# HGRN2 with a third operand buffer, and its steps spread differently over a head's four items

## The reference

```python
q = silu(q_raw) * DK ** -0.5
f = lb + (1 - lb) * sigmoid(z);  k = (1 - lb) * sigmoid(-z);  v = i_raw
b = cumsum(log f)                       # within a chunk
attn[t, s] = sum_d q[t, d] k[s, d] exp(b[t, d] - b[s, d])      # s <= t
o = attn @ v + (q * exp(b)) @ S         # S: state of the earlier chunks
o = rmsnorm(o, onorm_g);  y = o * silu(gate)
```

## Time and profile before

| | |
|---|---|
| median of 3 runs | 1422.78 us (1422.21 to 1424.14) |
| the profiled execution's own time | 1425.11 us |
| its span, first to last instruction | 1423.3 us |
| mean granted TensorE clock | 0.988 of full |
| TensorE matmul busy | 1303.7 us (92%), 5886 instructions |
| VectorE busy | 765.2 us (54%) |
| ScalarE busy | 639.7 us (45%) |
| GpSimd busy | 600.1 us (42%) |

### The profile page before, as it was taken

How to read it: one execution, slowest core, us unless ns; L and a number is a source line. 1 busy time by engine, 2 the same in 40 slices (tenths; PEclk the granted TensorE clock), 3 DMA queues, 4 the chain that set the end, 5 groups by cost and what they waited for, 6 DMA issues and landing times.

```text
span 1423.3 us, 16609 instructions
## 1 busy us (share of the span) xinstructions
PE 1303.7 (92%) x5886; PEld 1033.3 (73%) x5886; DVE 765.2 (54%) x1174; ACT 639.7 (45%) x988; POOL 600.1 (42%) x756
## 2 busy tenths in 40 slices
PE   0399889999999999999978988999999999999996
PEld 0277677788777777788857777778877777778884
DVE  6867884633555524534347778463355552454433
ACT  2245554544455334444335555454445533444531
POOL 3243333465232444445534333356523244454551
PEclk9999999999999999999989999999999999999998
DMA  9121111344223233333322111135422323333321
GB/s 366 45 75 60 59 45 59 104 157 131 83 68 110 91 108 100 103 126 104 104 83 74 60 58 49 57 104 162 132 77 67 111 94 111 98 102 123 105 103 59
DMA packets 46018, 139.70 MB, mean 98 GB/s; under 512 B 5744, under 2 KB 5744, under 8 KB 45680
## 3 DMA queue, kind: packets, MB, share of 16 engines
q1 hardware_dynamic: 28656, 102.65, 21.6%
q10 hardware_dynamic: 17280, 35.99, 7.9%
HBM read 136.52 MB, written 2.10 MB: 97 GB/s over the span
## 4 chain that ended last, share of the span: by engine, by line
PE 74%; DVE 14%; ACT 6%; issue 3%; DMA 1%; POOL 1%; ACTq 0%; DVEq 0%
PE ps_st L657 20%; PE ps_st L659 20%; PE ps_st L658 20%; PE ps_o L679 4%; PE ps_s L749 2%; PE ps_s L704 1%; PE ps_s L773 1%; DVE pro_acc L1125 1%; PE ps_w L758 1%; PE ps_misc L674 1%; ACT w_hi L833 1%; DVE t L1389 1%; DMA pro_w<-w_mod_first 1%; DVE h_lo L1394 1%; DVE hg_x L1334 1%
## 5 line engine op out<-in xcount | busy, mean ns | idle before, releaser
L570 POOL TENSOR_TENSOR w_lo<-raw,w_hi 128x256 fp32r<-128x256 f32 x744 | 587.9, 821 | 774.9 <-ACT w_hi L833 774.9
L657 PE MATMUL ps_st<-h_hi,w_hi 128*128 128x512 f32 x1008 | 413.4, 410 | 1.1 <-POOL w_lo L570 1.1
L659 PE MATMUL ps_st<-h_hi,w_lo 128*128 128x512 f32 x1008 | 395.0, 392 | 0.0
L658 PE MATMUL ps_st<-h_lo,w_hi 128*128 128x512 f32 x1008 | 394.2, 391 | 0.0
L657 PEld LDWEIGHTS ps_st<-h_hi,w_hi 128*128 128x128 f32 x1008 | 190.6, 189 | 48.5 <-issue 6.4
L658 PEld LDWEIGHTS ps_st<-h_lo,w_hi 128*128 128x128 f32 x1008 | 190.8, 189 | 43.7 <-issue 6.2
L659 PEld LDWEIGHTS ps_st<-h_hi,w_lo 128*128 128x128 f32 x1008 | 190.2, 189 | 41.3
L833 ACT ACTIVATE w_hi<-raw 128x1024 fp32r<-128x1024 f32 x186 | 195.2, 1051 | 27.6 <-PE ps_st L659 27.6
L855 ACT ACTIVATE gate_t<-gate_x 128x512 f32<-128x512 f32 x80 | 50.6, 632 | 248.3 <-DVE gate_x L1184 248.3
L1184 DVE TENSOR_SCALAR gate_x<-ps_st 128x512 f32<-128x512 f32 x80 | 55.2, 690 | 186.4 <-PE ps_st L659 186.0
L1532 DVE SCALAR_TENSOR_TENSOR mod_acc<-mod_w,cond,mod_acc 128x512 f32<-128x512 f32 x84 | 75.8, 902 | 21.2 <-DMA mod_w<-w_mod 18.5
(11 more groups left out here) (233 smaller groups left out, 1987.1 us busy)
## 6 DMA issues: line engine op xcount, KB each, us to landing
raw<-w_stream SPq DMA_DIRECT2D x186, 512.0 KB, 3.4
mod_w<-w_mod ACTq DMA_DIRECT2D x96, 256.0 KB, 2.7
pro_w<-w_mod_first ACTq DMA_DIRECT2D x16, 512.0 KB, 12.5
x<-x_t SPq DMA_DIRECT2D x4, 512.0 KB, 10.2
ret_decay<-decay ACTq DMA_DIRECT2D x2, 1024.0 KB, 5.9
out_t<-o_t SPq DMA_DIRECT2D x8, 256.0 KB, 2.1
cs<-cst SPq DMA_DIRECT2D x1, 906.5 KB, 4.8
pos_i<-positions ACTq DMA_DIRECT2D x1, 256.0 KB, 7.7
```

Of the source, the lines that this page charges most:

```text
L570: ins = nc.gpsimd.tensor_tensor(w_lo[:, i % RING, r], raw[:, i % RING, r], w_hi[:, i % RING, r].bitcast(F32), ALU.subtract)
L657: nc.tensor.matmul(dst[0:m, :], wh, hi, start=(k == 0), stop=False)
L658: nc.tensor.matmul(dst[0:m, :], wh, lo, start=False, stop=False)
L659: last = nc.tensor.matmul(dst[0:m, :], wl, hi, start=False, stop=(k == nk - 1))
```

## The change

The schedule of a head's steps is new. h is the head whose items run; what stands in a group before and after:

| group | before | after |
|---|---|---|
| f(h) | level steps 4, 5 of h-1 | level steps 2, 3 of h-1; value product of h-2 |
| q(h) | level steps 6, 7 of h-1; hz 1, 2; cross copy of h-1 | hz 1; level step 4 of h-1; hz 2; output of h-2 |
| i(h) | hz 3; value product of h-1; level steps 0, 1 of h; output of h-1 | hz 3; level steps 5, 6 of h-1 |
| g(h) | transposes of v; level steps 2, 3 of h | level step 7 and cross copy of h-1; transposes of v; level steps 0, 1 of h |

The steps of the last head run on through the first items of the latent attention. `hg_x` becomes three tiles, used by level modulo 3, and some tiles move to other addresses.

```diff
     def hg_first(h):
 
-        return ([("hg_lv", h - 1, 4), ("hg_lv", h - 1, 5)],
-                [("hg_lv", h - 1, 6), ("hg_lv", h - 1, 7), ("hz", h, 1), ("hz", h, 2), ("hg_cross", h - 1)],
-                [("hz", h, 3), ("hg_pv", h - 1), ("hg_lv", h, 0), ("hg_lv", h, 1), ("hg_out", h - 1)],
-                [("hg_v", h), ("hg_lv", h, 2), ("hg_lv", h, 3)])
+        return ([("hg_lv", h - 1, 2), ("hg_lv", h - 1, 3), ("hg_pv", h - 2)],
+                [("hz", h, 1), ("hg_lv", h - 1, 4), ("hz", h, 2), ("hg_out", h - 2)],
+                [("hz", h, 3), ("hg_lv", h - 1, 5), ("hg_lv", h - 1, 6)],
+                [("hg_lv", h - 1, 7), ("hg_cross", h - 1), ("hg_v", h), ("hg_lv", h, 0), ("hg_lv", h, 1)])
@@
     h = HG_HEADS
-    item("cq", 1)
-    s += hg_first(h)[0]
-    item("cq", 2)
-    s += [t for t in hg_first(h)[1] if t[0] != "hz"]
-    item("cq", 3)
-    s += [("hg_pv", h - 1)]
-    item("cq", 4)
-    s += [("hg_out", h - 1)]
+    tail = [[t for t in steps if t[0] not in ("hz", "hg_v") and t[1] < h] for steps in hg_first(h)]
+    for j in range(1, 5):
+        item("cq", j)
+        s += tail[j - 1]
     item("cq", 5)
+    s.append(("hg_pv", h - 1))
     item("ckv", 0)
     s.append(("cq_norm",))
     item("ckv", 1)
-    s.append(("cq_rest",))
+    s += [("hg_out", h - 1), ("cq_rest",)]
@@
-        hg_e, hg_x = at("hg_e", 12 * KB, [P, 2, SEQ]), at("hg_x", 16 * KB, [P, 2, SEQ])
-        hg_at = (at("hg_at0", 20 * KB, [P, CH, SEQ]), at("hg_at1", 40 * KB, [P, CH, SEQ]))
-        hg_kd = at("hg_kd", 28 * KB, [P, 3 * P])
+        hg_e, hg_x01 = at("hg_e", 12 * KB, [P, 2, SEQ]), at("hg_x", 16 * KB, [P, 2, SEQ])
+        hg_x2 = at("hg_x2", 87 * KB, [P, SEQ])
+        hg_x = (hg_x01[:, 0, :], hg_x01[:, 1, :], hg_x2[:])
+        hg_at = (at("hg_at0", 20 * KB, [P, CH, SEQ]), at("hg_at1", 28 * KB, [P, CH, SEQ]))
+        hg_kd = at("hg_kd", 85 * KB, [P, 3 * P])
@@
-        cq_raw, ckv_raw = at("cq_raw", 32 * KB, [P, CQT, SEQ]), at("ckv_raw", 44 * KB, [P, CKT, SEQ])
+        cq_raw, ckv_raw = at("cq_raw", 36 * KB, [P, CQT, SEQ]), at("ckv_raw", 79 * KB, [P, CKT, SEQ])
@@ tensor, level products
-                        left, right = (hg_x[:, n % 2, :], hg_x[:, n % 2, :]) if n < 5 else (hg_x[:, 0, :], hg_x[:, 1, :])
+                        left, right = (hg_x[n % 3], hg_x[n % 3]) if n < 5 else (hg_x[2], hg_x[0])
@@ vector, level_operands
-                    if 2 <= n < 5:
-                        dve.wait_ge(full[bank_of(("lv", h, n - 2))], e.use(full, ("lv", h, n - 2)))
+                    if 3 <= n < 5:
+                        dve.wait_ge(full[bank_of(("lv", h, n - 3))], e.use(full, ("lv", h, n - 3)))
                     elif n == 5:
+                        dve.wait_ge(full[bank_of(("lv", h, 2))], e.use(full, ("lv", h, 2)))
                         dve.wait_ge(full[bank_of(("lv", h, 3))], e.use(full, ("lv", h, 3)))
-                        dve.wait_ge(full[bank_of(("lv", h, 4))], e.use(full, ("lv", h, 4)))
-                    elif n < 2 and h:
+                    elif n < 3 and h:
                         dve.wait_ge(full[bank_of(("lv", h - 1, 5))], e.use(full, ("lv", h - 1, 5)))
...
```

More of the change, by code:

```diff
@@ L1331, in v @@
                             return t.rearrange("p (c s m) -> p c s m", s=2, m=LEVELS[n])
-                        V.tensor_tensor(v(hg_x[:, n % 2, :])[:, :, 0, :], v(hg_e[:, n % 2, :])[:, :, 0, :],
+                        V.tensor_tensor(v(hg_x[n % 3])[:, :, 0, :], v(hg_e[:, n % 2, :])[:, :, 0, :],
                                         v(k)[:, :, 0, :], ALU.mult)
-                        V.tensor_tensor(v(hg_x[:, n % 2, :])[:, :, 1, :], v(hg_e[:, n % 2, :])[:, :, 1, :],
+                        V.tensor_tensor(v(hg_x[n % 3])[:, :, 1, :], v(hg_e[:, n % 2, :])[:, :, 1, :],
                                         v(q)[:, :, 1, :], ALU.mult).then_inc(x_built, 1)
                     elif n == 5:
-                        V.tensor_tensor(hg_x[:, 0, :], hg_e[:, 0, :], k, ALU.mult)
-                        V.tensor_tensor(hg_x[:, 1, :], hg_e[:, 1, :], q, ALU.mult).then_inc(x_built, 1)
+                        V.tensor_tensor(hg_x[2], hg_e[:, 0, :], k, ALU.mult)
+                        V.tensor_tensor(hg_x[0], hg_e[:, 1, :], q, ALU.mult).then_inc(x_built, 1)
                     else:
```

## The result

The changed kernel takes 1446.03 us (median of 4 runs, 1444.91 to 1447.39) against 1422.52: the ratio is 1.0163, 95% interval 1.0146 to 1.0181. It is slower by 23.5 us, in the direction forecast (1430) but outside the range (to 1443), near the worst of the rivals (1445). The profiled execution took 1446.58 us, its span is 1444.7; the one of before 1425.11 and 1423.3. Beside the experiments the kernel before took 1423.70 to 1424.25 us, 1.2 to 1.7 more than beside the changed kernel, so a difference between the changed kernel and an experiment is uncertain by about that much, and reads low; the ratios to the kernel before are free of it.

A forecast was written before the change was run, and what follows sets the result against it. TensorE, busy 92% of the span, was taken as the bound, so reordering only changes its idle time. 42.4 - 37.4 - 6.3 + 8.4 = +7.1 us gave 1432.2, or 1430 on the median's scale; range 1414 to 1443.

The forecast's parts named there:

- the worst of the rivals: All six gaps trip the clock at the longest price and every pair is slow: +22, 1445 us; chance 0.15.
- Step 1, the buffer: Third operand tile for level operands: VectorE never waits there, so alone worth 0 (bounds -1 to +1 us).
- Step 2, the start: First level product of a layer: its 2.8 to 3.0 us wait shrinks to 0.9 per layer (bounds 0 to 3).
- Steps 3 and 4, the new wait and the loop: Transposes of v wait for w0's copy, looping over VectorE's drain of g: 7.2 us in heads 2 and 3, 5.3 in head 1.
- the walk: Engine-by-engine timing of head 2 or 3 from one drain of g to the next: cycle 39.8 against 37.4 us.
- The waits outside the loop: Per layer, 0.9 at the start and 0.6 for the tail's cross operands; also 1.2 at level 5 in head 1.
- My 42.4 us: TensorE's HGRN2 waits after the change, both layers, 21.2 per layer; bounds 16 to 48 us.
- the 37.4 for the kernel before: The 20 waits at level and cross-chunk products before, 34.4 us listed, plus about 0.15 us each for the emptied pipeline.
- Step 5, the slow rate: VectorE's base operands beside GpSimd's work, taken at the upper end; at the lower end a cycle is 0.9 us shorter.
- Step 6, the tail: Head 3's output moves to ckv1 from cq4, still several items ahead of its reader: 0 (bound 0 to +1).
- The clock: Half clock after TensorE's gaps: 6.3 us saved from three old drops, 8.4 added by four gaps in heads 2 and 3.
- +7.1: Net change forecast for the whole kernel in us, from new and old waits and clock losses.

The follow-up runs named there:

- e4: Kernel before with only the third operand tile and its waits, order unchanged: 1424.41 us, ratio 1.0006 to the kernel before.
- e3: Changed kernel with unused matmuls in TensorE's gaps ahead of the transposes of v and the cross products: 1438.34 us, ratio 1.0099 to the kernel before.
- e1: Changed kernel with the transposes of v written to bank o in place of w0: 1419.62 us, ratio 0.9966 to the kernel before.
- e5: Changed kernel with transposes of v moved from the fourth item's group to the next head's first, bank w0 kept: 1423.9 us, ratio 0.9995.
- e6: e5 with the output of h-2 listed behind the third item: 1414.29 us, ratio 0.9931 to the kernel before.
- e7: e5 with head 3's output directly behind its value product at cq5, ahead of the c_q norm: 1418.4 us, ratio 0.9959.
- e9: Changed kernel with transposes of v as in e5, head 3's output as in e7, output of h-2 behind the fourth item: 1401.18 us, ratio 0.9845.
- e10: Kernel before with unused matmuls in its gaps (level 4's product, cross products, a layer's first level product): 1420.71 us, ratio 0.9976.

## Why the prediction was right in direction and wrong in size

- *Step 1, the buffer*: right, 0 (e4).
- *Step 2, the start*: there is no listed wait at the first level product, where I took 0.9 (and 3.0 + 4 - 5.9 is 1.1, not 0.9); the clock stays full over 92 to 102. Right to about 1 us a layer.
- *Steps 3 and 4, the new wait and the loop*: right, and in size. At full clock the cycle is the 39.8 us of the walk (e3). Forecast were 2.5 and 4.7 us in heads 2 and 3, 4.1 in head 1, none in head 0, six waits on ScalarE's copy. Measured are 2.6 and 4.6 in layer 1, 4.1 in head 1; in layer 0 the wait on the copy is 3.2, because the cross products ahead of it run at half clock. e1 and e5 show the mechanism, e6 the part of the output chain.
- *The waits outside the loop failed in part.* Head 0's base operands I had not walked at all: 2.0 us a layer. The cross products of the last head, in the tail, I put at 0.6: 2.2. Against that the 0.9 of the start and the 1.2 at level 5 in head 1 did not come. My 42.4 us counts from the end of one matmul's pitch to the next start, like the 37.4 for the kernel before; on that scale the 14 listed waits of after are 42.9 + 14 times 0.15 = 45.0. So 2.6 us are missing, and the nearness of 42.4 and the listed 42.9 is luck.
- *Step 5, the slow rate*, is half in the trace: of the two base operands one, L1337, took 1.24 us, the other, L1336, 0.69. I took both at the upper end. In their place the exponents behind them (L1310) took 0.96 and not 0.56, so the stretch came to 2.8 us (158.41 to 161.25) where the walk has 2.9.
- *Step 6, the tail, failed.* "Still several items ahead of the product that reads it: 0". True of the product, but the step has other neighbours: its column sum takes bank misc ahead of the ckv norm's, and its root stands in ScalarE's queue behind the rest of the c_q norm. 4.8 us of waits and 3.0 us of half clock, about 8 us; e7 gives 7.9.
- *The clock was mis-sized.* For the kernel before I took 6.3 us from one trace; the filler gives 3.2. After, 8.4 were forecast for the heads and 7.7 found (9 by the ratios), but as six falls and not four, each cheaper than the 2.1 us I gave it: the sum came out by luck. The six falls are what the Trainium skill, "TensorE: Matmul & The Clock Gate", section "HAM oscillation — how this bites in real kernels", would have, and the trace agrees, with a granted clock of 0.57 to 0.72 behind each; I gave the nearer row (769 to 773 at full clock) more weight than it bore. Net 2.4 us, 3.8 by the ratios.

The corrections, 2.6 + 8 + 2.4, bring +7.1 to +20.1, and to 21.5 with the ratios' price of the clock, against 21.4 between the two spans; the terms themselves are known to a microsecond or two, so the last tenths are chance. The medians differ by 23.5, because the profiled execution of before stood 2.6 above its median and that of after 0.6 above. The worst rival's 1445 was near by other terms: the waits were not the 48 us it assumed, its clock cost of 18 us was twice the one found in the heads, and it had no tail.

## What to carry to other kernels

When steps are put in another order, list for each both neighbours on every shared resource: the last user of its bank and who frees it, and the next user; a copy that was an item away can end up behind a drain that stands behind everything else. Put a chain that only has to be done some time (here the output) where its engine waits anyway; moved to another place it mostly changes which product waits (15 us at the cross products in e5, 12 at level 2 in e6). TensorE's HGRN2 waits fell from 22.0 us (e5) to 18.4 (e6) and 12.8 (e9). And walk the first head and the last as well as the steady ones: the 2.0 and 2.2 us a layer that I missed are there.

## What the runs showed of the hardware

Half clock came after gaps of about 2 us only sometimes (3 of the 20 waits in the trace of before) and its cost on the mean was 3.2 us in the kernel before (e10), but after each of the six waits at the transposes in the changed one (4.1 us in head 1; in heads 2 and 3 3.2 to 4.6 us, behind a wait of 2.6 and the cross products). Unused matmuls in the gaps kept the granted clock at 1.00 there and made the kernel 7.7 us faster, though they did nothing. A base operand of 128x512 (L1337) took 1.24 us beside GpSimd's weight subtractions, where the same instruction took 0.68 in all eight heads of the kernel before; the one just ahead of it (L1336), under the same four subtractions (157.09 to 160.85), took 0.69, so overlap alone does not slow every such instruction.
